# The bias over compressed keys: 240 small products of a one-hot table, or four products over shifted pieces of a stored row

## What is computed

```python
cmp_end = jnp.arange(n_cmp) * CMP_STRIDE + CMP_LEN - 1      # 16 j + 31
dist_c = pos[:, None] - cmp_end[None, :]
s = s + jnp.transpose(tab_g[t5_bucket(dist_c)], (0, 2, 3, 1))[None]
p_cmp, _ = masked_softmax(s, (dist_c >= 0)[None, :, None, None, :])
```

## Time and profile before

| what | value |
|---|---|
| time, median of 3 runs | 3437.22 us (3434.15 to 3437.6) |
| the profiled execution's time | 3434.16 us |
| its span | 3432.3 us |
| TensorE busy | 3063.7 us, 89% of the span |
| VectorE / ScalarE / GpSimd busy | 1604.9 / 1004.0 / 597.5 us |
| mean granted TensorE clock | 0.916 of 2.4 GHz |
| stage of the even projection | up to 581 us |

### The profile page before, as it was taken

One profiled execution on the slowest core, in us unless ns is written; L12 is line 12 of the kernel. 1 busy time (PEld: TensorE's weight loads), 2 busy tenths in 40 slices (PEclk: granted clock), 3 DMA queues, 4 the chain that ended last, 5 costly groups with the idle time before them and its releaser, 6 DMA issues. The chain is left out here.

```text
span 3432.3 us, 62164 instructions
## 1 busy us (share of the span) xinstructions
PE 3063.7 (89%) x22097; PEld 2000.3 (58%) x22097; DVE 1604.9 (47%) x4215; ACT 1004.0 (29%) x2384; POOL 597.5 (17%) x953
## 2 busy tenths in 40 slices
PE   7999997899998999997868759899978877999978
PEld 4455445899997555564635534566645655666633
DVE  3100111688885366564435556422156654555523
ACT  1000000343442466663213311100045542444411
POOL 0000000333330000002036634000011113333200
PEclk9999999899999599996769879999989997999989
DMA  5543372766662223134659954633132118999751
GB/s 176 213 145 128 133 262 83 159 157 157 152 158 57 77 64 82 54 99 111 259 177 297 304 201 144 206 128 106 42 92 80 52 31 298 352 354 350 264 211 74
DMA packets 334608, 556.49 MB, mean 162 GB/s; under 512 B 70994, under 2 KB 217626, under 8 KB 330618
## 3 DMA queue, kind: packets, MB, share of 16 engines
q1 hardware_dynamic: 251900, 343.56, 32.3%
q0 software_dynamic: 54256, 174.12, 16.0%
q10 hardware_dynamic: 28148, 34.82, 3.0%
HBM read 490.59 MB, written 118.25 MB: 177 GB/s over the span
## 5 line engine op out<-in xcount | busy, mean ns | idle before, releaser
L344 PE MATMUL PS<-even_w,even_xT 128*128 128x512 f32 (+1 forms) x1152 | 488.1, 582 | 2.4 <-DMA even_w<-in_w_in_e 2.4
L1147 ACT ACTIVATE cmp_xT<-PS 64x512 f32<-64x512 f32 x260 | 154.1, 593 | 750.4 <-PE PS L1236 748.9
L344 PEld LDWEIGHTS PS<-even_w,even_xT 128*128 128x128 f32 x1152 | 219.5, 193 | 252.9 <-issue 247.0
L344 PE MATMUL PS<-odd_w,odd_xT 128*128 128x368 f32 x896 | 288.8, 478 | 1.4 <-DVE odd_xT L293 1.4
L1268 PE MATMUL PS<-cmp_xd,cmp_w 128*128 128x256 f32 (+1 forms) x1088 | 258.9, 377 | 0.0
L300 DVE COPY even_o<-PS 128x512 f32<-128x512 f32 (+3 forms) x81 | 50.4, 622 | 438.1 <-PE PS L344 424.2
L344 PEld LDWEIGHTS PS<-odd_w,odd_xT 128*128 128x128 f32 x896 | 168.9, 193 | 100.2 <-issue 5.0
L1147 DVE COPY cmp_xT<-PS 64x512 f32<-64x512 f32 x260 | 179.1, 689 | 65.8 <-PE PS L1236 61.1
L1268 PEld LDWEIGHTS PS<-cmp_xd,cmp_w 128*128 128x128 f32 x1088 | 195.5, 193 | 20.3
L1167 POOL DMA_DIRECT2D cmp_pairs<-in_cache_nsa x256 | 151.5, 599 | 310.3 <-issue 299.7
L1950 POOL DMA_DIRECT2D s_fox_kv<-in_cache_fox x256 | 137.7, 538 | 263.0 <-PE PS L2234 208.4
(11 more groups left out here) (457 smaller groups left out, 5198.8 us busy)
## 6 DMA issues: line engine op xcount, KB each, us to landing
s_fox_kv<-in_cache_fox POOLq DMA_DIRECT2D x256, 256.0 KB, 7.2
s_fox_kv<-in_cache_fox SPq DMA_DIRECT2D x256, 256.0 KB, 8.1
cmp_pairs<-in_cache_nsa SPq DMA_DIRECT2D x256, 128.0 KB, 4.0
cmp_pairs<-in_cache_nsa POOLq DMA_DIRECT2D x256, 128.0 KB, 4.2
s_sel_kv<-in_cache_nsa POOLq DMA_DIRECT2D x256, 128.0 KB, 5.0
s_sel_kv<-in_cache_nsa SPq DMA_DIRECT2D x256, 128.0 KB, 5.2
out_dil_sample<-in_cache_dil_w SPq DMA_DIRECT2D x8, 4088.0 KB
even_w<-in_w_in_e SPq DMA_DIRECT2D x8, 2048.0 KB, 8.1
```

What stands on the lines that cost most here:

```text
L344: last = nc.tensor.matmul(bank(c, t, 128)[:, 0:n], xT[:, k, t * 128:t * 128 + 128], w[:, c % WS, k, 0:n], start=(k == 0), stop=(k == KT - 1))
L1147: last = nc.vector.tensor_copy(dst, x) if l else nc.scalar.activation(dst, x, ACT.Copy)
```

## The change

The one-hot table of the compressed bias goes, with its two loads and its 240 products. In its place GpSimd reads pieces of the stored bias row back from DRAM: for product m and half h, head `2 m + h`, partition q gets 993 values from position 31 + q of the row of that head (`far`), which is the bias of the distance `992 - q - y` at place y. Taken at every sixteenth place (63 of them), and with the partitions reversed by `E.flip`, this is the table for two heads: one product of 126 columns. The four products stand at jobs 15, 17, 24 and 26 (`FAR`). `far` has two buffers; the loads for m = 0 and 1 are issued behind the third row store, with a wait for the second to have landed, those for m = 2 and 3 behind the last row store, each with a wait for the product that frees its buffer. VectorE copies all 504 columns at once at job 27, and it writes the places from 63 on to -1e30 once, before job 0 (`first`).

```diff
--- before.py
+++ after.py
@@ -79,9 +79,6 @@
                              (d < WIN, d >= 0, d <= 128)] +
                             [one_hot(d * dil, (d >= 0) & (d <= w // dil)) for w, dil in DILATIONS[1:]], 1).astype(np.float32)
 
-    u = np.arange(120)
-    d = i[None] - 16 * (u[:, None] - 56) - 31
-    c["oh_cmp_p"] = one_hot(d, d >= 0)
     t = np.arange(4)[None, :, None]
     key = i[None, None, :]
     new_d = t - key
@@ -555,27 +552,37 @@
 
     KINDS = ((0, 0, 8), (1, 0, 8), (2, 8, 4), (3, 12, 4), (4, 16, 4))
     CUTS = ((0, 512), (512, 1024), (1024, 1152))
+    FAR = (15, 17, 24, 26)
 
     def __init__(self, nc, E, name, sb, sem, junk, o):
         self.nc, self.E, self.junk = nc, E, junk
-        self.oh, self.ohc = sb("oh", [33, 5, 1152]), sb("ohc", [33, 60, 128])
+        self.oh, self.far = sb("oh", [33, 5, 1152]), sb("far", [128, 2, 2, 16 * 63])
         self.r, self.cmp_b = sb("r", [8, 2, 1152]), sb("cmp_b", [128, 8, 120])
-        (self.oh_in, self.ohc_in, self.row_mm, self.row_ok, self.cmp_mm, self.cmp_ok, self.cmp_out) = map(sem, (
-            "oh_in", "ohc_in", "row_mm", "row_ok", "cmp_mm", "cmp_ok", "cmp_out"))
-        self.row_out = [sem(f"row_out{x}") for x in range(2)]
+        (self.oh_in, self.row_mm, self.row_ok, self.cmp_mm, self.cmp_ok, self.cmp_out) = map(sem, (
+            "oh_in", "row_mm", "row_ok", "cmp_mm", "cmp_ok", "cmp_out"))
+        self.row_out, self.far_in = ([sem(f"{n}{x}") for x in range(2)] for n in ("row_out", "far_in"))
 
     def gpsimd(self, pool):
         E = self.E
         pool.dma_start(self.oh[:], E.c_oh_rows).then_inc(self.oh_in, 16)
-        pool.dma_start(self.ohc[:], E.c_oh_cmp_p[:, 0:60]).then_inc(self.ohc_in, 16)
+
+        def far(m):
+            for h in range(2):
+                v = E.rows[8 + 2 * m + h:9 + 2 * m + h, 31:31 + 16 * 62 + 1]
+                pool.dma_start(self.far[:, m % 2, h, 0:16 * 62 + 1], bass.AP(v.tensor, v.offset, [[1, 128], [1, 16 * 62 + 1]])).then_inc(self.far_in[m % 2], 16)
         at = 0
         for k, _, nh in self.KINDS:
             pool.wait_ge(self.row_ok, 3 * k + 3)
             pool.dma_start(E.rows[at:at + nh, :], self.r[0:nh, k % 2]).then_inc(self.row_out[k % 2], 16)
+            if k == 2:
+                pool.wait_ge(self.row_out[1], 16)
+                far(0)
+                far(1)
             at += nh
-        pool.wait_ge(self.cmp_mm, 4)
-        pool.dma_start(self.ohc[:], E.c_oh_cmp_p[:, 60:120]).then_inc(self.ohc_in, 16)
-        pool.wait_ge(self.cmp_ok, 2)
+        for m in range(2, 4):
+            pool.wait_ge(self.cmp_mm, m - 1)
+            far(m)
+        pool.wait_ge(self.cmp_ok, 1)
         pool.dma_start(E.cmp_rows.rearrange("h p u -> p h u"), self.cmp_b[:]).then_inc(self.cmp_out, 16)
         pool.wait_ge(self.row_out[0], 48)
         pool.wait_ge(self.row_out[1], 32)
@@ -595,14 +602,12 @@
             hold(self.row_ok, job - 1)
             at = 512 * (job % 2)
             nc.tensor.matmul(E.PS[0:nh, at:at + b - a], E.tabx[:, h0:h0 + nh], self.oh[:, k, a:b], start=True, stop=True).then_inc(self.row_mm, 1)
-        elif job < 23:
-            m = job - 15
-            hold(self.ohc_in, 16 * (m // 4 + 1))
+        elif job in self.FAR:
+            m = self.FAR.index(job)
+            hold(self.far_in[m % 2], 32 * (m // 2 + 1))
             hold(self.row_ok, 15)
-            for u in range(15 * (m % 4), 15 * (m % 4) + 15):
-                at = 512 * (m // 4) + 8 * u
-                last = nc.tensor.matmul(E.PS[:, at:at + 8], self.ohc[:, u, :], E.tabx[:, 0:8], start=True, stop=True)
-            last.then_inc(self.cmp_mm, 1)
+            nc.tensor.matmul(E.PS[:, 126 * m:126 * m + 126], E.flip[:], self.far[:, m % 2].rearrange("p h (u x) -> p h u x", x=16)[:, :, :, 0],
+                             start=True, stop=True).then_inc(self.cmp_mm, 1)
 
     def vector(self, dve, job):
         V, E = self.nc.vector, self.E
@@ -615,13 +620,12 @@
             dve.wait_ge(self.row_mm, job + 1)
             at = 512 * (job % 2)
             V.tensor_copy(self.r[0:nh, k % 2, a:b], E.PS[0:nh, at:at + b - a]).then_inc(self.row_ok, 1)
-        elif job in (19, 23):
-            x = (job - 19) // 4
-            dve.wait_ge(self.cmp_mm, 4 * x + 4)
-            V.tensor_copy(self.cmp_b[:, :, 60 * x:60 * x + 60], E.PS[:, 512 * x:512 * x + 480].rearrange("p (u h) -> p h u", h=8)).then_inc(self.cmp_ok, 1)
+        elif job == self.FAR[-1] + 1:
+            dve.wait_ge(self.cmp_mm, 4)
+            V.tensor_copy(self.cmp_b[:, :, 0:63], E.PS[:, 0:504].rearrange("p (h u) -> p h u", h=8)).then_inc(self.cmp_ok, 1)
 
     def first(self, dve):
-        pass
+        self.nc.vector.memset(self.cmp_b[:, :, 63:120], NEG)
 
     def scalar(self, act, job):
         pass
```

## The result

The changed kernel takes 3371.01 us (median of 4 runs, 3370.35 to 3384.12) against 3435.68 for the kernel before (4 runs, 3428.19 to 3437.6): a ratio of 0.9825, 95% interval 0.98 to 0.985. In all, ten runs of the changed kernel have a mean of 3376.9 us and 45 of before 3431.4 us: 54.5 us apart, with a spread of one run of 6 to 8 us in either.

What follows compares the result with a forecast made beforehand. TensorE was taken to bound the changed stage: 46.7 us removed less 2.0 and 0.2 added is 44.5 us, from 3434.16 to 3389.7, plus 1.3 for the runs' median: 3391 us, range 3384 to 3402.

Steps and rivals of the forecast that it cites:

- TensorE bounds the stage, and what leaves its list leaves the time: Even projection stage: TensorE has one 7.5 us wait behind the start; other engines follow, so work removed there shortens the time.
- Groups, 27.5 us, and changeovers, 1.5: Stretch from 204.91 us: eight groups of 15 one-hot products at 3.44 us each, plus eight changeovers of 0.19, all removed.
- The new products, 2.0 + 0.2 us: Four added 126-column products: 0.31 us plus 0.19 changeover each, and 0.2 together for reading every sixteenth value.
- The loads, nothing: Eight new 496 KB loads on GpSimd land before the products need them, so they cost no time.
- The wait, 7.5 us: TensorE's wait at L604 for the second half of the one-hot table, removed by the change.
- the rest, 11.5 us, is clock and changeover: Remainder of the guest's 46.5 us in that stretch: slow tiles and groups at low clock, plus changeovers; all removed.
- the clock is not given back: Rival, chance 0.05: low clock belongs to the stretch of time, not the small products; only 34.5 us go, 3401 us.
- the sum: Net saving ahead of 317 us: 46.7 removed less 2.0 and 0.2 added, 44.5 us; later stages just move.
- The range: Whole time 3384 to 3402 us, from the downstream case up to the first two rivals.

Runs made afterwards that it cites:

- b_dense: b_nowait with each group of 15 one-hot products replaced by four products of 512 columns with full 128x128 weights; 3413.37 us, ratio 0.994.
- b_nowait: The kernel before with its second four groups of one-hot products three jobs later, all 240 products kept; 3422.62 us, ratio 0.9976.
- b_63: The kernel before with 63 one-hot products in place of 240, in four groups at jobs 15 to 18, from one load; 3402.19 us, ratio 0.9907.

## Why the prediction was off

- **TensorE bounds the stage, and what leaves its list leaves the time**: right, in every profile.
- **Groups, 27.5 us, and changeovers, 1.5**: right. An undisturbed group lasts 3.51 us in every profile of before, and in b_dense eight groups of the same length, at full clock, cost 564.2 - 535.9 = 28.3 us.
- **The new products, 2.0 + 0.2 us**: measured 0.42 + 0.50 + 0.41 + 0.50 = 1.8 us, and a changeover of 0.09 ahead of the first (198.19 to 205.16 is 6.97 us), 2.2 together if all four pay it. The parts were not right: a contiguous one is 0.2 and not 0.31, and the step of sixteen adds 0.2 each, where I had derived 0.08 from the weight load at the same step. They happened to cancel.
- **The loads, nothing**: right. They landed in 7.9 to 12.9 us and had 50 to 57.
- **The wait, 7.5 us**: seen at 7.5 to 8.0 us in the three executions with a low price of the clock, and at 2.1 and 2.6 in the two with a high one, with a mean of 5.6. There the tile ahead of it is slower, and the table lands sooner after its issue (11.1 and 11.6 us against 14.3 to 14.8).
- **The step that failed is the term for the clock, "the rest, 11.5 us, is clock and changeover".** It was the remainder of one execution, and so added up to the stage's end of that execution by construction. Without the 1.5 of changeover it is 10.0 us; five executions show 10.5 to 26.7 with a mean of 17.7 (9.8 to 26.1 with a mean of 16.3 by the stretch alone), and the one I had was the lowest, or within 0.2 us of it. With the means, the clock more by 7 and the wait less by 2, the stage gives 588.2 - 538.1 = 50.1 us instead of 44.5. I priced the clock as if a group had a fixed cost; the rival that I set beside it (the clock is not given back) lay on the wrong side, and none let it cost more. That the first pair of profiles gave 44.3 us is no proof of the sum: before's was the very profile that the sum was made from, and the changed kernel's stage hardly varies (537.7 to 538.6).
- **The 20 us between forecast and result**, worked out: 5.6 us are that term. 4.1 are the level of before, 3431.4 as the mean of 45 runs, where I started at 3435.5. 5.9 are luck: the first four runs of the changed kernel, whose median is that much below the mean of ten. The 4.4 us left are the gap of 54.5 less the 50.1 of the stage; with five and three profiles, and ten runs at a spread of 7.5, that is within what these means can tell, and no run shows a cause for it. The rest of the span behind the stage is 2844.7 us as a mean of before's five profiles and 2840.6 of the three of the changed kernel's form (2830.8, 2846.5, 2844.5): 4 us again, inside a scatter of 16.
- **The range** failed with it. I took the three runs of before, 3434.15 to 3437.6, for the spread of the kernel; 45 runs lie from 3419.91 to 3448.42. It is not luck alone: the mean of all ten runs of the changed kernel, 3376.9, lies below the range too. From the level of 3431.4 the forecast would have been 3386.9, and 3381.3 with the stage's 50.1.

What stays open: why one execution pays 10 us and another 27 for the same groups, how many columns hold the clock and what part the weights have in it, and what brought b_dense 10 us above its stage's share.

## What to carry to other kernels

Products of a few columns cost TensorE more than their own time: beside 27.5 us of products stood 10 to 27 us of tiles and groups at a low clock, and the second number can't be read off one profile. Before pricing a change by a term of clock, look at several executions, or replace the suspect by dense work of the same length, as b_dense did: in the stage this takes the clock out and leaves the rest. And a sum that fits one execution to the tenth says nothing of its spread.

## What the runs showed of the hardware

- One core, one program: 3419.91 to 3448.42 us over 45 runs on several chips, with mean granted clocks of 0.911 to 0.922 in the 41 of them that were run beside the experiments.
- Groups of 15 back-to-back products of 8 columns lower the granted clock (0.78 to 0.91 over 204 to 330 us in the profiles of before), and they do so without a wait: 0.88 in b_nowait and in b_63, where TensorE is busy for all of the 126 us. Products of 128 columns with 33-row weights still do at times (0.96); products of 512 columns with full weights at the same places do not (1.00).
- What the same eight groups cost in low clock varies from 10 to 27 us between five executions of one program, while the stage without them ends within 0.9 us of itself in three.
- A product of 126 float32 columns read at every sixteenth value takes 0.42 us to the start of the next tile, a contiguous one 0.22.
- Eight loads of 128 overlapping pieces, each shifted by one value (3972 bytes from one row of 4608), issued by GpSimd, land in 7.9 to 12.9 us (7.2 to 13.1 over all four profiles with them), two to four at a time and amid other traffic.
